# Latent attention: one engine for the gate chunk's low part, and seven gate tiles ahead of each step's first scores

## The reference, cut to what matters

```python
def mla_mixer(h, positions, w_in, q_norm_g, kv_norm_g, w_uq, w_uk, w_uv, w_out):
    proj = h @ w_in
    q_c, kv_c, k_r, z = jnp.split(proj, [256, 384, 448], axis=-1)       # z: 2048 wide
    ...                                                                   # norms; q from q_c; rope
    q_lat = jnp.einsum('bshd,rhd->bshr', q_nope, w_uk)
    ...
        s = jnp.einsum('bqhr,bkr->bhqk', ql, kv_c) + jnp.einsum('bqhd,bkd->bhqk', qr, k_rope)
        s = s.astype(jnp.float32) * ATTN_SCALE
        p = jax.nn.softmax(jnp.where(mask, s, -jnp.inf), axis=-1).astype(kv_c.dtype)
        return jnp.einsum('bhqk,bkr->bqhr', p, kv_c)
    ...
    o = jnp.einsum('bshr,rhd->bshd', o_lat, w_uv).reshape(B, S, MLA_WIDTH)
    return (o * jax.nn.silu(z)) @ w_out
```

## Time and profile before

| | us |
|---|---|
| median of 3 runs (1784.82 to 1784.94) | 1784.92 |
| the profiled execution | 1785.65 |
| its span, first to last instruction | 1783.9 |
| TensorE busy in it | 1746.5 |
| VectorE, ScalarE, GpSimd busy | 1130.3, 828.7, 695.5 |

### The profile page before, as it was taken

One profiled execution on the slowest core, in us unless ns is written; L12 is line 12 of the kernel. 1 busy time (PEld: TensorE's weight loads), 2 busy tenths in 40 slices (PEclk: granted clock), 3 DMA queues, 4 the chain that ended last, 5 costly groups with the idle time before them and its releaser, 6 DMA issues.

```text
span 1783.9 us, 29617 instructions
## 1 busy us (share of the span) xinstructions
PE 1746.5 (98%) x10544; PEld 1530.9 (86%) x10544; DVE 1130.3 (63%) x1944; ACT 828.7 (46%) x1405; POOL 695.5 (39%) x841
## 2 busy tenths in 40 slices
PE   8999999999999999999999999999998999999998
PEld 7888888878878778899899999888965899999887
DVE  7777754676676645898487776313667387876312
ACT  4323321566555633545365555324547455555322
POOL 0000046221010261765366666453423266666461
PEclk9999999999999999999999999999999999999999
DMA  9544654212112143234324343422311124343321
GB/s 368 178 135 149 199 198 175 87 42 74 38 53 62 48 153 95 72 104 132 95 72 118 94 112 111 139 97 76 130 48 48 48 79 111 95 116 94 130 95 71
DMA packets 195572, 193.72 MB, mean 109 GB/s; under 512 B 10912, under 2 KB 167328, under 8 KB 195488
## 3 DMA queue, kind: packets, MB, share of 16 engines
q1 hardware_dynamic: 195056, 192.19, 34.2%
q10 hardware_dynamic: 432, 0.42, 0.1%
HBM read 190.48 MB, written 2.10 MB: 108 GB/s over the span
## 4 chain that ended last, share of the span: by engine, by line
PE 71%; issue 14%; POOL 6%; DVE 5%; ACT 3%; DMA 1%; SPq 0%; POOLq 0%; DVEq 0%; ACTq 0%
PE PS L2262 23%; PE PS L2264 22%; PE PS L2263 22%; POOL slot_low L720 2%; POOL w_low L751 2%; POOL w_low L737 1%; PE PS L2369 1%; ACT w_high L849 1%; POOL gate_sum_a L704 1%; DMA w_raw<-in_o_w_out 1%; POOL h_sum_low L710 1%; DVE masked L2204 1%; PE PS L2892 0%; PE PS L2880 0%; DVE x L1674 0%
## 5 line engine op out<-in xcount | busy, mean ns | idle before, releaser
L737 POOL TENSOR_TENSOR w_low<-w_raw,w_high 128x256 fp32r<-128x256 f32 x333 | 274.2, 858 | 568.9 <-ACT w_high L849 543.2
L720 POOL TENSOR_TENSOR slot_low<-w_raw,slot_high 128x256 fp32r<-128x256 f32 x400 | 318.7, 822 | 176.2 <-ACT slot_high L1208 173.2
L849 ACT ACTIVATE w_high<-w_raw 128x2048 fp32r<-128x2048 f32 (+2 forms) x86 | 157.5, 1831 | 307.9 <-PE PS L2264 286.5
L2262 PE MATMUL PS<-h_high,w_high 128*128 128x512 f32 (+1 forms) x688 | 246.8, 359 | 3.9 <-POOLq L755 1.6
L2263 PE MATMUL PS<-h_low,w_high 128*128 128x512 f32 (+1 forms) x688 | 241.0, 350 | 0.0
L2264 PE MATMUL PS<-h_high,w_low 128*128 128x512 f32 (+1 forms) x688 | 240.9, 350 | 0.0
L2262 PE MATMUL PS<-h_sum_high,slot_high 128*128 128x256 f32 x800 | 227.0, 284 | 4.5 <-DVE joined L2018 3.3
L2264 PE MATMUL PS<-h_sum_high,slot_low 128*128 128x256 f32 x800 | 226.4, 283 | 0.0
L2263 PE MATMUL PS<-h_sum_low,slot_high 128*128 128x256 f32 x800 | 226.4, 283 | 0.0
L2262 PE MATMUL PS<-h_high,slot_high 128*128 128x256 f32 x600 | 170.1, 284 | 1.9 <-ACT PS L1222 1.9
L2263 PE MATMUL PS<-h_low,slot_high 128*128 128x256 f32 x600 | 169.8, 283 | 0.0
(11 more groups left out here) (376 smaller groups left out, 4084.4 us busy)
## 6 DMA issues: line engine op xcount, KB each, us to landing
w_raw<-in_f_gate_up SPq DMA_DIRECT2D x88, 512.0 KB, 5.0
w_raw<-in_f_down SPq DMA_DIRECT2D x40, 512.0 KB, 4.1
w_raw<-in_e_w_in SPq DMA_DIRECT2D x32, 512.0 KB, 6.7
gains<-in_ada_t SPq DMA_DIRECT2D x16, 1024.0 KB, 5.0
w_raw<-in_a_w_in SPq DMA_DIRECT2D x24, 512.0 KB, 4.9
w_raw<-in_o_w_in SPq DMA_DIRECT2D x20, 512.0 KB, 4.6
ada_raw<-in_ada_t SPq DMA_DIRECT2D x16, 512.0 KB, 11.5
w_raw<-in_e_w_out SPq DMA_DIRECT2D x16, 512.0 KB, 4.6
```

Source lines behind the costliest of these rows:

```text
L720: ins = nc.gpsimd.tensor_tensor(slotL[j][:, piece], src[:, piece], slotH[j][:, piece].bitcast(F32), ALU.subtract)
L737: ins = nc.gpsimd.tensor_tensor(WL[s][:, piece], raw[s][:, piece], WH[s][:, piece].bitcast(F32), ALU.subtract)
L849: nact(WH[s][:, 0:n], raw[s][:, 0:n], ACT.Copy).then_inc(w_high[s], 1)
L2262: mm(dst, lh, rh, start=first, stop=False, skip_group_check=True)
```

## The change

VectorE makes the whole low part of the next gate chunk, 2048 columns in one instruction, waits for its own result, and hands back the raw buffer; GpSimd's loop and the two semaphores between the two engines are gone. And the default table `Z` puts seven gate tiles ahead of score(0) instead of four. From score(1) to turn 0 there is then one tile instead of two, from turn 0 to turn 1 one instead of two, from turn 2 to turn 3 one instead of two; from turn 3 on the table is as it was.

```diff
--- before.py
+++ after.py
@@ -199,7 +199,6 @@
 UNITS = KVH * T
 SLICE = 256
 CREDIT = 1
-Z_DVE = 1024
 
 
 def program(nc, a, out):
@@ -396,7 +395,7 @@
             sem(n) for n in ("proj_done", "qa_ready", "kv_ready", "qr_ready", "qn_ready"))
         s_done, m_ready, e_ready, p_ready, t_done, pT_ready, pv_done, sz_ready, oz_ready = (
             sem(n) for n in ("s_done", "m_ready", "e_ready", "p_ready", "t_done", "pT_ready", "pv_done", "sz_ready", "oz_ready"))
-        z_dve, z_pool, kraw_ready = sem("z_dve"), sem("z_pool"), sem("kraw_ready")
+        kraw_ready = sem("kraw_ready")
         oh_ready, ol_ready, q2_half = sem("oh_ready"), sem("ol_ready"), sem("q2_half")
         k2_step, kd_ready, v2_ready = (sem(n) for n in ("k2_step", "kd_ready", "v2_ready"))
         q2_raw, q2_turn, q2_ready, q2_sin, q2_cos = (sem(n) for n in ("q2_raw_ready", "q2_turn", "q2_ready", "q2_sin", "q2_cos"))
@@ -741,19 +740,9 @@
 
                 first, last = 0, pairs - (name in BOUNDARY)
                 if name == "mla":
-                    first = last
                     low(0, 0, MLA_CHUNK)
                     low(0, 1)
-                    with pool.Fori(0, 7) as i:
-                        pool.wait_ge(w_high[1], i + (B.split[1] + 2))
-                        for c in range(Z_DVE, CHUNK, SLICE):
-                            piece = slice(c, c + SLICE)
-                            ins = nc.gpsimd.tensor_tensor(WL[1][:, piece], raw[1][:, piece], WH[1][:, piece].bitcast(F32), ALU.subtract)
-                        ins.then_inc(z_pool, 1)
-                        pool.wait_ge(z_pool, i + 1)
-                        pool.wait_ge(z_dve, i + 1)
-                        pool.sem_inc(w_split[1], 1)
-                        pool.sem_inc(raw_free[1], 1)
+                    continue
                 if name in SHARED:
                     pool.wait_ge(w_high[0], B.split[0] + 1)
                     for c in range(0, SHARED_AT, SLICE):
@@ -1850,7 +1839,9 @@
                     norm(u)
                 def gates_low():
                     dve.wait_ge(w_high[1], i + (BASE["mla"].split[1] + 2))
-                    v.tensor_tensor(WL[1][:, 0:Z_DVE], raw[1][:, 0:Z_DVE], WH[1][:, 0:Z_DVE].bitcast(F32), ALU.subtract).then_inc(z_dve, 1)
+                    v.tensor_tensor(WL[1][:, :], raw[1][:, :], WH[1][:, :].bitcast(F32), ALU.subtract).then_inc(w_split[1], 1)
+                    dve.wait_ge(w_split[1], i + (BASE["mla"].split[1] + 2))
+                    dve.sem_inc(raw_free[1], 1)
 
                 if more:
                     fold_split(i + 1)
@@ -2563,7 +2554,7 @@
                              start=(k == 0), stop=(k == T - 1), skip_group_check=True)
                 ins.then_inc(pv_done, 1)
 
-            def attend(i, Z=(0, 4, 7, 9, 10, 12, 14, 15, 15, 16, 16)):
+            def attend(i, Z=(0, 7, 9, 10, 11, 12, 14, 15, 15, 16, 16)):
                 pe.wait_ge(w_split[1], B.split[1] + i + 1)
                 pe.wait_ge(sz_ready, i + CREDIT)
```

## The result

The changed kernel takes 1791.88 us (median of 5 runs, 1791.63 to 1792.18) against 1784.92 us: 7.0 us slower, a ratio of 1.0039 with a 95% interval of 1.0028 to 1.0050. The forecast was 1791.6 us. The profile shows the mechanism that it named: both stalls are where it put them.

The account below looks back on a forecast made before the run. TensorE, busy 98% of the span, was taken as the bound. Per step, +1.55 us to the first score and -0.59 to turn 3 make +0.96; seven steps give 6.7 us, so 1791.6 us, range 1786 to 1796.

Parts of the forecast that it names:

- The wait for GpSimd: Ahead of each step's first gate matmul: removing TensorE's wait for the gate chunk's low part gains 0.51 us a step.
- rival c: At the step's start: the loop's turn holds TensorE anyway, so the wait stays; 1795.2 us, chance 0.06.
- VectorE's delay and its cover: Before the first score: VectorE's later work comes 1.06 us later, hidden by seven tiles with 1.1 us of cover left.
- Second score to turn 0: Up to the first probabilities' transpose: the chain takes 2.04 us, so the tile taken away there saves nothing.
- Turn 0 to turns 1 and 2: After the first transpose: turn 1 follows after 1.74 us and turn 2 after 5.27, both without a wait.
- Turn 3: VectorE's chain puts it 9.68 us behind the second score, so only 0.59 of 2.06 us come back.
- Restarting after the second stall: Behind the stall ahead of turn 3: TensorE's restart was taken at nothing.
- (a): Whole step: TensorE's work ends last everywhere, moved tiles cost nothing, GpSimd waits vanish; 1781.4 us, chance 0.06.
- (b): Only turn 0 waits because the chain to turn 3 catches up; +1.2 us in all, 1786.1 us, chance 0.10.
- (d): Between turns 0 and 3: stalls lower TensorE's clock to 1.2 GHz; 43 us more, about 1835 us, chance 0.02.
- The time outside the stage: Outside the latent attention stage: time unchanged.

Follow-up runs that it names:

- the table alone: The kernel before with seven tiles ahead of the first score and the low part still shared with GpSimd: 1795.74 us.
- the low part alone: The changed kernel with the old table, four tiles ahead of the first score: 1788.66 us.
- The early gating: The changed kernel with VectorE's two gating products of the previous step's heads moved ahead of the first maximum: 1785.55 us.
- the one with 1536 columns: The kernel before with VectorE making 1536 low-part columns, GpSimd 512, and five tiles ahead of the first score: 1782.65 us.

## Why the prediction was right, point by point

**The wait for GpSimd.** Forecast 0.51 us a step. With the wait gone the first gate matmul follows after 0.22 us and the first score after 478.23 - 473.24 = 4.99 us, forecast 5.03 (476.37 - 471.34); the pair of runs with the new table gives 0.55 a step. The bound at zero (rival c) is out, because the table alone is 3.9 us slower than the table with the new low part.

**VectorE's delay and its cover.** Forecast 1.06 us later and 1.1 us of cover left; the low part for the first score now ends 7.37 us after the chunk's low part starts, 6.36 before, so 1.01 later, and 1.1 us remain. Without the tiles the score waits, as forecast, and the low part alone is slower than the kernel before.

**Second score to turn 0.** Forecast 2.04 us with one tile as with two, read off step 0; measured 2.04, with 0.59 us idle.

**Turn 0 to turns 1 and 2.** Forecast 1.74 and 5.27 us without a wait; measured 1.75 and 5.25 without a wait.

**Turn 3.** Forecast 9.68 us behind the second score; measured 9.69, with 0.66 us idle, and the link named as the cause (the gating of the previous heads) is the one whose move takes the stall away.

**The term that was too small, and the one that was too large.** Restarting after the second stall was taken at nothing. From turn 3 to the last query matmul it is 505.73 - 489.17 = 16.56 us; the kernel before has 502.84 - 486.35 = 16.49, where 486.35 is in the earlier trace rows and 502.84 is this row of the kernel before:

```profile
502.84 0.39 PE L2264 MATMUL PS<-qc_high,fold_low 128*128 128x512 f32 x1
```

So restarting costs 0.07 us a step, 0.5 us in all. In step 3 of the five kernels with a stall ahead of turn 3 (the table of all kernels has them with 9.69 or 9.09 us) the distance is 16.55 to 16.57 us, whether the stall is of 0.66 us or of 0.1; in the four without one it is 16.49 to 16.51. The early gating is one of these four, and so it gave back 0.87 us a step and not 0.75 to 0.8. The rows of before held a sign of it: after the wait for GpSimd the first gate tile takes 472.77 - 471.98 = 0.79 us and the next ones 0.685. In the other direction the first score came 0.04 us a step earlier than forecast (4.99 for 5.03), 0.3 us in all. With both, 6.7 us become 6.9, against 7.0 measured. The two partly cancel, so part of the forecast's nearness is luck.

**The rivals.** (a), that TensorE's work ends last everywhere, asked for a gain of 3.5 us and for a chain of under 1.35 us to turn 0 and under 8.2 us to turn 3; they took 2.04 and 9.69, and the new table alone lost 10.9 us. (b), that only turn 0 waits, is the state of the kernel with the early gating, 0.7 us above the kernel before where (b) was priced at 1.2, and not that of the changed kernel. The prediction held against (b) that VectorE has no idle time there; the cover did exist, 1.13 us ahead of the first maximum, but the order of VectorE's instructions made no use of it. (d), a lower clock, was priced too low: two of the three moved tiles, not all three, come from between turns 0 and 3, so 8.23 - 2 x 0.685 = 6.86 us of work would have taken twice as long, 48 us more in seven steps and not 43. The lower clock did not come: the two stretches with the stalls, in the changed kernel, have the granted clock of 1.00, the 2.4 GHz level:

```profile
480.00:482.00 2.00, 1.41 (x8) 0.93 (x8) 1.30 (x7) 0.77 (x5) 0.00 (x0) 1.00 0.00 0
488.00:490.00 2.00, 1.34 (x10) 0.91 (x9) 1.21 (x5) 1.00 (x4) 0.00 (x0) 1.00 0.00 0
```

The swing of the clock that the Trainium skill tells of in "TensorE: Matmul & The Clock Gate", section "A second HAM failure mode: psum-queue depth-cycling", did not happen here with idle gaps of 0.59 and 0.66 us in a step of 32.5 us.

**The time outside the stage.** It was forecast as unchanged. The medians differ by 7.0 us, but the profiled executions only by 6.0 (1791.63 and 1785.65), although the first matmul of the output product behind the stage comes 7.2 us later in the changed kernel's (632.22 against 625.03). From there to the start of the last matmul the profiled execution of before takes 1152.70 us, that of the changed kernel 1151.49, and those of the seven other kernels 1151.45 to 1152.00. So the profiled execution of before is the odd one. Three waits of TensorE make most of the 1.2 us: 0.84 us for 0.55 on GpSimd (at 648.82), 0.96 for 0.78 on VectorE (at 775.13) and 0.91 for 0.33 on GpSimd (at 1473.80). Why they were longer in that execution stays open.

## What to carry to other kernels

Filler work that an in-order engine does while it waits for another has value only at the place where it waits: a gate tile of 0.685 us was worth nothing ahead of turn 0 and all of its time between turns 0 and 1. Before moving it, take from the trace the other engines' distance from their last dependence to each place (here 2.04 and 9.69 us) and compare it with the work that remains. When a wait is removed by making another engine's instruction longer, follow that engine's order to the next thing it releases. And where a chain ends last, first ask which link need not be in it: here two gating products, put into an idle place a few instructions earlier, gave back 6.3 of the 7.0 us that the change had cost.

## What the runs showed of the hardware

GpSimd's first piece of each chunk hardly ran beside VectorE's instruction, which the prediction did not consider. A piece of 256 columns takes 0.73 us behind the end of that instruction; the first one, which starts 0.05 us after VectorE's low part (two operands in SBUF), takes 1.78 us when that is 1.23 us long, and 2.32 us when it is 1.76 us long (1536 columns). First the kernel before, then the one with 1536 columns; min, median and max of the pieces, where the max is the first piece:

```profile
L751 POOL TENSOR_TENSOR w_low<-w_raw,w_high x28: 730/738/1780, 404.9 to 597.0; 128x256 fp32r<-128x256 f32 x28
```

```profile
L751 POOL TENSOR_TENSOR w_low<-w_raw,w_high x14: 728/1528/2318, 404.9 to 594.0; 128x256 fp32r<-128x256 f32 x14
```

The timeline of that kernel, GpSimd's pieces and VectorE's instruction:

```profile
467.16 3.01 POOL L751 TENSOR_TENSOR w_low<-w_raw,w_high 128x256 fp32r<-128x256 f32 x2 [28.11 <-ACT w_high L849]
...
467.11 1.76 DVE L1853 TENSOR_TENSOR w_low<-w_raw,w_high 128x1536 fp32r<-128x1536 f32 x1 [0.29 <-ACT w_high L849]
```

In both the first piece ends 0.60 us after VectorE's instruction. So VectorE's half and GpSimd's first piece were done nearly one after the other. The 3.87 us that the prediction set against VectorE's 1.23 hold that standstill; four pieces of 0.73 us make 2.92. The whole chunk is ready 3.92 us after VectorE's start in the kernel before and 3.06 us with 1536 columns on VectorE. The Trainium skill, "SBUF — State Buffer", section "SBUF: two separate sides", says that the two engines share a port pair which one of them holds for a whole instruction while the other stands still; these rows agree, but for some 0.1 us that still overlaps. VectorE takes longer beside GpSimd, too, though here the two are only seen together and no run separates them: in step 7 of the kernel before GpSimd makes the next stage's low parts (from 616.75) while VectorE normalises, and the products that take 0.42 and 0.49 us in step 3 take longer:

```profile
617.69 0.70 DVE L1828 TENSOR_SCALAR probs<-probs,soft 128x384 f32<-128x384 f32 x1
...
620.47 0.86 DVE L1828 TENSOR_SCALAR probs<-probs,soft 128x512 f32<-128x512 f32 x1
```
